# Down bias added by a product at the head of each expert block, and one expert block moved from second place to near the end

## The reference, cut to what matters

```python
def moe(x2, w_router, b_router, w_gate_up, b_gate_up, w_down, b_down):
    logits = (x2 @ w_router + b_router).astype(jnp.float32)
    top_v, top_i = lax.top_k(logits, TOP_K)              # 4 of 32
    gates = jax.nn.softmax(top_v, axis=-1)
    ...                                                  # tokens sorted by expert, in blocks
    def expert_block(args):
        xe, e = args
        gu = xe @ w_gate_up[e] + b_gate_up[e]            # 1024 x 2048
        gate, up = gu[:, :D_FF], gu[:, D_FF:]
        gate = jnp.minimum(gate, SWIGLU_LIMIT)
        up = jnp.clip(up, -SWIGLU_LIMIT, SWIGLU_LIMIT)
        h = gate * jax.nn.sigmoid(SWIGLU_ALPHA * gate) * (up + 1.0)
        return h @ w_down[e] + b_down[e]                 # 1024 x 1024
    ...
    return jnp.sum(y * gates[..., None].astype(y.dtype), axis=1)
```

## Time and profile before

| | us |
|---|---|
| median of three runs | 1329.43 |
| profiled execution | 1329.48 |
| its span, first to last instruction | 1327.6 |
| PE busy | 1227.2 (92%) |
| DVE busy | 826.2 (62%) |
| ACT busy | 608.1 (46%) |
| POOL busy | 147.5 (11%) |

### The profile page before, as it was taken

The page is one execution under the profiler, slowest core; times in us unless marked ns, Lnnn a source line. Parts: engine busy times, 40 slices in busy tenths (PEclk is TensorE's granted clock), DMA queues, the critical chain, the costliest instruction groups (busy, mean ns, idle before and its releaser), DMA issues.

```text
span 1327.6 us, 18587 instructions
## 1 busy us (share of the span) xinstructions
PE 1227.2 (92%) x6270; PEld 792.3 (60%) x6273; DVE 826.2 (62%) x1333; ACT 608.1 (46%) x822; POOL 147.5 (11%) x170
## 2 busy tenths in 40 slices
PE   7999999989999899999999999999999999999971
PEld 5888864467564647847474736574747747474620
DVE  3896758699382929929282837292829928374703
ACT  4111242387272727826263635272636736354502
POOL 9100012010000000000001010100010010101011
PEclk9999999989999999999999999999999999999987
DMA  9620178389999999999999999899999999999994
GB/s 320 92 42 1 38 231 335 130 297 402 354 416 411 419 412 418 413 407 418 408 419 400 419 391 375 320 416 417 419 411 420 393 386 419 408 421 382 424 401 179
DMA packets 67295, 457.49 MB, mean 345 GB/s; under 512 B 15758, under 2 KB 19538, under 8 KB 34456
## 3 DMA queue, kind: packets, MB, share of 16 engines
q1 hardware_dynamic: 56344, 435.28, 80.5%
q0 software_dynamic: 10880, 21.30, 6.8%
HBM read 439.99 MB, written 23.24 MB: 349 GB/s over the span
## 4 chain that ended last, share of the span: by engine, by line
PE 38%; DMA 21%; DVE 14%; issue 4%; ACT 2%; DVEq 0%; SPq 0%; ACTq 0%; POOLq 0%
PE bank L2270 20%; DMA ring_lo<-in_w_gate_up 17%; PE bank L2410 13%; DVE w_lo L2554 11%; DMA w_out<-in_w_down 4%; ACT w_hi L2048 1%; PE bank L2421 1%; DVE cmix L2572 1%; PE bank L2253 1%; PE bank L2260 1%; DVE h_lo L2567 1%; PE bank L2360 1%; DVE cmix L2575 1%; PE bank L2430 0%; DMA x<-token_sums 0%
## 5 line engine op out<-in xcount | busy, mean ns | idle before, releaser
L2554 DVE TENSOR_TENSOR w_lo<-ring_lo,w_hi 128x1024 fp32r<-128x1024 f32 x271 | 316.6, 1218 | 93.7 <-ACT w_hi L2048 91.7
L2048 ACT ACTIVATE w_hi<-ring_lo 128x1024 fp32r<-128x1024 f32 x271 | 271.1, 1052 | 86.4 <-DMA ring_lo<-in_w_gate_up 60.1
L2410 PE MATMUL bank<-ring_lo,x_s 128*64 128x512 f32 x832 | 187.4, 597 | 0.0
L2270 PE MATMUL bank<-w_hi,x_hi 128*128 128x512 f32 x544 | 175.2, 404 | 9.8 <-DVE x_lo L2560 7.7
L2270 PE MATMUL bank<-w_lo,x_hi 128*128 128x512 f32 x544 | 169.8, 393 | 0.0
L2270 PE MATMUL bank<-w_hi,x_lo 128*128 128x512 f32 x544 | 169.1, 392 | 0.0
L2554 DVE TENSOR_TENSOR w_lo<-w_out,w_hi 128x1024 fp32r<-128x1024 f32 x136 | 161.5, 1217 | 5.8 <-ACT w_hi L2048 5.7
L2048 ACT ACTIVATE w_hi<-w_out 128x1024 fp32r<-128x1024 f32 x136 | 141.1, 1055 | 30.8 <-PE bank L2270 30.7
L1943 POOL DMA_INDIRECT token_sums<-ymix,row_cur x32 | 54.0, 1688 | 725.7 <-ACT ymix L2078 700.3
L2270 PEld LDWEIGHTS bank<-w_hi,x_hi 128*128 128x128 f32 x544 | 99.1, 190 | 44.0 <-issue 19.4
L2410 PEld LDWEIGHTS bank<-ring_lo,x_s 128*64 128x64 f32 x832 | 56.2, 136 | 102.4 <-issue 100.5
(11 more groups left out here) (473 smaller groups left out, 1445.6 us busy)
## 6 DMA issues: line engine op xcount, KB each, us to landing
ring_lo<-in_w_gate_up SPq DMA_DIRECT2D x128, 2048.0 KB, 19.1
w_out<-in_w_down SPq DMA_DIRECT2D x128, 1024.0 KB, 20.7
ring_lo<-in_w_in SPq DMA_DIRECT2D x3, 2048.0 KB, 20.9
w_out<-in_w_out SPq DMA_DIRECT2D x2, 2048.0 KB, 9.6
x<-in_x_prompt SPq DMA_DIRECT2D x6, 512.0 KB, 11.6
ring_lo<-in_w_in SPq DMA_DIRECT2D x2, 1024.0 KB, 9.9
token_sums<-x SPq DMA_DIRECT2D x4, 512.0 KB
ffn_in<-hf SPq DMA_DIRECT2D x4, 512.0 KB, 5.5
```

Of the source, the lines that this page charges most:

```text
L2048: nc.scalar.activation(high(j), raw(j), ACT.Copy).then_inc(s["w_hi"], 1)
L2270: last = nc.tensor.matmul(bank[b + u][:], v[:, k, :], part(j)[:, u, :], start=(j == 16 and first), stop=(k == KD - 1 and part is high and ...
L2410: last = nc.tensor.matmul(bank[2 * half][64 * u:64 * u + 64, :], x_s[:, k % 4, 64 * (k // 4):64 * (k // 4) + 64], gu[:, k, :, half, 256 * ...
L2554: v.tensor_tensor(low(j), raw(j), high(j).bitcast(F32), ALU.subtract).then_inc(s["w_lo"], 1)
```

## The change

It has two parts.

**The down bias.** The gates' copies, their transposes, the ten products, ACT's copies over `x`, and POOL's five accumulating transfers are gone. Instead POOL splits `b_down` into three bf16 parts together with the gate/up bias (`bq` and `bparts` are 768 columns wide instead of 512, eight loads instead of four), stores them to HBM (`down_bias`, four more stores), and SP loads all 96 rows (3 parts of 32 experts) into a part of `x` that is free by then, ahead of the last two pieces of the first expert's weights. A 96 x 32 matrix `pick96` has, in the column of an expert, ones in the three rows of that expert. For each block DVE copies the expert's column to `picked_row` (`open_next`), and PE opens the block's down sums with a product of this column, broadcast over the slots, and the 96 bias rows (`open_down`): two bf16 matmuls of 512 columns for a wide or a small block, four of 256 for a quarter and for the rest beside position 16. The down products that follow no longer start the sums but add to them.

**The order.** The wide block at position 1 is gone from there: position 1 is now the small block of the first pair, and all that follows stands one position earlier. A wide block (`THIRD_EXTRA`, the smallest of the wide experts) stands at position 29, behind the last pair and ahead of the two quarters. The kinds and their numbers are as before, and so are the eight pieces of each expert and the rules for their issue.

```diff
-FIRST_EXTRA = 2 + 2 * PAIRS[0]
+FIRST_EXTRA = 1 + 2 * PAIRS[0]
...
-FINAL = SECOND_EXTRA + 2 + 2 * PAIRS[3]
+THIRD_EXTRA = SECOND_EXTRA + 1 + 2 * PAIRS[3]
+FINAL = THIRD_EXTRA + 2
...
+def down_rows(keep):
+
+    region = keep["x"][0:3 * E, NT - 1, :]
+    return tuple(region[:, o:o + n].bitcast(BF16) for o, n in ((0, D // 2), (D // 2, E // 2), (D // 2 + E // 2, 1)))
...
@@ router, SP @@
-        for c in range(P // E):
-            sp.dma_start(bdn[c * E:(c + 1) * E, :], a["b_down"][0]).then_inc(bdn_in, 16)
...
         sp.wait_ge(e["x_in"], 16)
+        sp.wait_ge(s["down_set"], 16 * 4)
+        sp.dma_start(down_rows(keep)[0], scratch["down_bias"].rearrange("r e c n -> (r e) (c n)")).then_inc(dn_in, 16)
         for j in range(6, LOADS):
             weight_load(sp, a, keep, mid, 0, j).then_inc(keep["landed"][j], 16)
@@ router, POOL @@
         for c in range(4):
-            pool.dma_start(bq[c * E:(c + 1) * E, :], a["b_gate_up"][0][:, c * 512:(c + 1) * 512]).then_inc(s["bias_in"], 16)
+            pool.dma_start(bq[c * E:(c + 1) * E, 0:512], a["b_gate_up"][0][:, c * 512:(c + 1) * 512]).then_inc(s["bias_in"], 16)
+            pool.dma_start(bq[c * E:(c + 1) * E, 512:768], a["b_down"][0][:, c * 256:(c + 1) * 256]).then_inc(s["bias_in"], 16)
...
+        pool.wait_ge(acc_set, acc_set0 + 16 * NT)
+        pool.wait_ge(s["fold"], 2)
+        g.tensor_copy(down_rows(keep)[1], pick96[:])
+        g.tensor_copy(down_rows(keep)[2][:, 0:1], pick96[:, 0:1]).then_inc(e["picked"], 1)
@@ experts, POOL @@
-        for q in range(3):
-            add_bias(q)
-        gather(1)
-        for q in range(3, NT):
-            add_bias(q)
-        pool.wait_ge(keep["bd_added"], 16 * NT)
+        gather(1, 2)
+        acc_set, acc_set0 = keep["spent"]["acc_set"]
+        pool.wait_ge(acc_set, acc_set0 + 16 * NT)
         scatter(0, 0)
@@ experts, PE @@
+        def open_down(b, parts=1):
+
+            n, step = P // parts, D // parts
+            for c in range(max(parts, 2)):
+                o, w = (0, 512) if parts == 1 else (n * c, step)
+                nc.tensor.matmul(bank[b + c if parts == 1 else b][o:o + n, 0:w], picked_row[:, 0:1].to_broadcast([3 * E, n]),
+                                 down_bias[:, c * w:(c + 1) * w], start=True, stop=False)
...
                 if j == 16:
+                    pe.wait_ge(s["y_free"], q + 1)
+                    open_down(4)
                     pe.wait_ge(s["h_lo"], 2 * lq + 1)
-                    pe.wait_ge(s["y_free"], q + 1)
...
-        wide(0, 0, expert_at(pe, 1), 1)
-        wide(1, 1, expert_at(pe, 2), 2)
+        wide(0, 0, expert_at(pe, 1), 2, True)
...
-        pair(3, PAIRS[3] - 1, 4)
+        pair(3, PAIRS[3] - 1, 1)
+        wide(THIRD_EXTRA, SMALL_RANK - 1, expert_at(pe, FINAL - 1), 4)
@@ experts, DVE @@
+        def open_next(e):
+
+            v.tensor_copy(picked_row[:, 0:1], pick96[:, bass.ds(e, 1)])
...
                 elif j == 23:
                     take_h(q, 1)
+                    open_next(e_next)
```

More of the change, by code:

```diff
@@ L1137, in router @@
     rest = buf("rest", [P, NT, E])
-    gate4 = buf("gate4", [P, NT, P // E, E])
-    gT = buf("gT", [P, NT * P])
-    bdn = buf("bdn", [P, D])
+    pick96 = buf("pick96", [3 * E, E], BF16)
     gsum = buf("gsum", [P, NT])
@@ L1179, in router @@
     keep["landed"] = [sem(f"landed{j}") for j in range(LOADS)]
-    keep["loop"] = {n: sem("e_" + n) for n in "onehot idx x_in xT_psum x_hi x_lo w_hi w_lo sel_psum bias_used".split()}
+    keep["loop"] = {n: sem("e_" + n) for n in "onehot idx x_in xT_psum x_hi x_lo w_hi w_lo sel_psum bias_used picked".split()}
     e = keep["loop"]
@@ L1275, in _ @@
         for c in range(4):
-            pool.dma_start(scratch["bias"][:, c], bparts[c * E:(c + 1) * E]).then_inc(s["bias_set"], 16)
+            pool.dma_start(scratch["bias"][:, c], bparts[c * E:(c + 1) * E, :, 0:512]).then_inc(s["bias_set"], 16)
+        for c in range(4):
+            pool.dma_start(scratch["down_bias"][:, :, c].rearrange("r e n -> e r n"), bparts[c * E:(c + 1) * E, :, 512:768]).then_inc(s["down_set"], 16)
         pool.wait_ge(s["bias_set"], 16 * 4)
+        pool.wait_ge(s["down_set"], 16 * 4)
         pool.wait_ge(s["mm"], 4 * NT)
@@ L1472, in _ @@
         x_transposes(Q)
-        pe.wait_ge(s["gate4"], Q)
-        for q in range(Q):
-            last = nc.tensor.transpose(bank[0][:, q * P:(q + 1) * P], gate4[:, q].rearrange("p c e -> p (c e)"), ident[:])
-        last.then_inc(s["gT_psum"], 1)
         strips(Q)
@@ L1479, in _ @@
         logits(Q)
-        pe.wait_ge(s["gT"], 1)
-        pe.wait_ge(bdn_in, bdn_in0 + 16 * (P // E))
-        for j in range(4):
-            bias_rows(j)
         ranks(Q)
@@ L1493, in _ @@
         last.then_inc(s["first_psum"], 1)
-        for j in range(4, 2 * Q):
-            bias_rows(j)
-        pe.wait_ge(s["gate4"], NT)
-        pe.wait_ge(keep["bd_sb"], 3)
-        nc.tensor.transpose(bank[3][:, 0:P], gate4[:, Q].rearrange("p c e -> p (c e)"), ident[:]).then_inc(s["gT_psum"], 1)
         pe.wait_ge(s["extra"], 1)
@@ L1501, in _ @@
         nc.tensor.matmul(bank[7][0:E, NT * E + 1:NT * E + 2], tri[0:E, 0:E], extra_b[:], start=True, stop=True).then_inc(s["upto_psum"], 1)
-        pe.wait_ge(s["gT"], 2)
-        for j in range(2 * Q, 2 * NT):
-            bias_rows(j)
         pe.wait_ge(s["held"], 1)
@@ L1515, in _ @@
                 last = nc.tensor.transpose(bank[XT_BANK[h]][:, (k % 4) * P:(k % 4 + 1) * P], xg[:, k * P:(k + 1) * P], ident[:])
-            last.then_inc(s["gT_psum"] if h == 0 else e["xT_psum"], 1)
-        pe.wait_ge(keep["bd_sb"], 9)
+            last.then_inc(s["x0_psum"] if h == 0 else e["xT_psum"], 1)
+        pe.wait_ge(s["x_new"], 2 * NT)
         pe.wait_ge(bias_in, bias_in0 + 64)
@@ L1809, in experts @@
     row_parts = {(n, c): scratch[n].rearrange("t (c d) -> (t c) d", c=c) for n in ("hf", "acc") for c in (1, 2, 4)}
+    down_bias, pick96, picked_row = down_rows(keep)
     def raw(j):
@@ L2012, in _ @@
         scatter_rest()
-        scatter(TOP, 0)
+        scatter(TOP, 1)
         with pool.Fori(0, PAIRS[2] - 1) as i:
-            pair(2, i, 1)
-        pair(2, PAIRS[2] - 1, 1, 1)
+            pair(2, i, 0)
+        pair(2, PAIRS[2] - 1, 0, 1)
         gather(SECOND_EXTRA + 1, 2)
         added(SECOND_EXTRA - 1)
-        scatter(SECOND_EXTRA, 1)
+        scatter(SECOND_EXTRA, 0)
         with pool.Fori(0, PAIRS[3] - 1) as i:
-            pair(3, i, 0)
-        pair(3, PAIRS[3] - 1, 0, 4)
+            pair(3, i, 1)
+        pair(3, PAIRS[3] - 1, 1, 1)
+        gather(THIRD_EXTRA + 1, 4)
+        added(THIRD_EXTRA - 1)
+        scatter(THIRD_EXTRA, 1)
         gather(FINAL, 4)
@@ L2179, in _ @@
             split(1, 0, j, first=True)
-        wide(0, 0, 0, 1, 1)
-        wide(1, 1, 1, 2, 2)
+        wide(0, 0, 0, 2, 1)
         def pair(run, i, side, next_parts=2):
@@ L2269, in products @@
                 for u in range(2):
-                    last = nc.tensor.matmul(bank[b + u][:], v[:, k, :], part(j)[:, u, :], start=(j == 16 and first),
+                    last = nc.tensor.matmul(bank[b + u][:], v[:, k, :], part(j)[:, u, :], start=False,
                                             stop=(k == KD - 1 and part is high and not first))
             last.then_inc(s["w_used"], 1)
+        def open_down(b, parts=1):
[4 more added lines that the diff above has]
+                                 down_bias[:, c * w:(c + 1) * w], start=True, stop=False)
         def set_bias(q):
@@ L2305, in set_bias_small, with wide @@
             last.then_inc(s["bias_used"], 1)
-        def wide(q, lq, e_next, next_parts):
+        def wide(q, lq, e_next, next_parts, first=False):
             pe.wait_ge(s["x_lo"], lq + 1)
@@ L2689, in _ @@
             split(0, j)
-        wide(0, 0, 0, expert_at(dve, 1), 1, blocks_back=0)
-        wide(1, 1, 1, expert_at(dve, 2), 2, 0)
+        wide(0, 0, 0, expert_at(dve, 1), 2, 0, blocks_back=0)
         def pair(run, i, side, next_parts=2):
```

172 lines of the change are left out of this document (74 added, 98 removed).

## The result

The changed kernel takes 1331.1 us (median of 18 runs, 1329.1 to 1334.8) where the kernel before, run beside it, takes 1328.23 (18 runs, 1327.02 to 1330.65): a ratio of 1.0022, 95% interval 1.0016 to 1.0029. The forecast was 0.9 us faster; it came out 2.9 us slower. The time lies in the range; the direction is wrong. The profiled execution (1333.17 us, span 1331.3) is one of the longer ones, by 2.1 us against the median; one part of the reason is shown further down.

The account below looks back on a forecast made before the run. The loop was taken as bound by DMA weight loads (411 GB/s), by compute where their share falls. Terms -0.7 + 1.5 - 0.2 - 2.2 + 0.7 = -0.9 gave 1328.5 us against the median; range 1324.5 to 1332.5.

Parts of the forecast that it names:

- Term B: Router: POOL's wider, later split holds up DVE, +1.5 us, between -2.7 and +5.5.
- term A: Router: without ten bias products the rank product starts sooner and DVE's `cum` waits less, -0.7 us, at most 0.98.
- the prediction's own sign: Router: PE's `x` transposes start about 1.5 us after 226.18; 224 or below means "faster", 229 or above "blocked in full on DVE".
- blocked in full on DVE: Router: every two-SBUF DVE step of the first tile ends only with a POOL step; +3.5, total 1330.6 us, chance 0.19.
- C: Block 0: four transposes instead of eight, one more short DVE step, two opening products; -0.2 us, between -0.5 and +0.5.
- D: Block order: position 1's wide block (35.8 us) goes, an extra wide near the end costs 33.6; -2.2 us.
- E: Opening products in other blocks: hidden by loads except at the largest expert's block and its rest; +0.7 us.
- faster: Rival: split's loss on DVE doesn't grow (-0.7), extra wide block costs less (-3.6); sum -4.5, 1325.0 us, chance 0.28.
- load queue: Rival: at position 29 the next load has lost its lead, leaving a gap; sum +4.2, 1333.7 us, chance 0.09.
- the products count: Rival: the loop is bound by PE, so opening products cost 14 us in all; about 1342 us, chance 0.04.

Follow-up runs that it names:

- the later turning: Changed kernel with the turning of the next block's token rows, ahead of the largest expert's block, moved behind two more pieces of down products: ratio 1.0012.
- the new order with the narrow split late: Kernel before with the new block order, POOL's adding transfers kept, and its 512-column gate/up split moved behind the sixth half tile of x: 0.9970, 1325.25 us.
- the whole split late: Changed kernel with POOL's whole split, gate/up and down bias together (768 columns), moved behind the sixth half tile of x: ratio 0.9975.

## Why the prediction was wrong

**Term B, the split, was the step that failed**, in its size: +1.5 was taken, +3.4 to +3.8 came. To the loop's start the old router needs 82.1 us (mean of 82.63 and 81.63), the router of the changed kernel 85.5 (mean of 85.06, 85.77, 85.99 with the later turning, 85.19), 3.4 more. To the end of the projections, where term A has no part yet, the same executions need 62.65 and 66.44 in the mean, 3.8 more. The prediction saw that "the steps also start later, since eight loads are to land and not four" and gave it half a microsecond; the trace of before already had four loads landing 0.8 to 1.5 us apart, and with the four more the start came 9.6 us later, out of the tables and into the chain of gates. There 4.5 to 5.3 us were lost in place of 1.6 to 1.8 (2.7 had been estimated). The rest, about 0.7 us from the sixth half tile to the end of the projections, goes with the half clock behind PE's 4.12 us wait, a consequence no term had: PE turns `x` at 228.42, 0.72 us after DVE's `x` is there, and before 0.06 us after it. By the prediction's own sign, PE's turning of `x` stands 3.3 us later behind the router's first instruction than before, which would be 229.5 for the 226.18 of the earlier trace rows, past the 229 named for the rival "blocked in full on DVE". By its size (+3.5) this is that rival, and its mechanism is the one seen; of the steps it named, two on `row` were held and `hf` was not, and casts and steps of the gates were held that it had not named.

**Term A, the bias products ahead of the rank product, was 0 at full clock, not -0.7.** The 0.98 us that `cum` waited in the earlier trace rows belong to one execution in which the clock had fallen. Its window, then the same place in the execution with the new order only, whose router is the same:

```profile
259.00:262.00 3.00, 3.00 (x11) 0.61 (x10) 2.04 (x9) 1.06 (x2) 0.00 (x0) 0.69 0.46 179
```

```profile
257.00:259.60 2.60, 2.54 (x11) 0.82 (x11) 2.36 (x9) 1.09 (x3) 0.00 (x0) 1.00 0.35 139
```

```profile
257.36 2.10 PE L1457 MATMUL bank<-bdn,gT 32*24 32x512 f32 x8
259.49 0.19 PE L1449 MATMUL bank<-mask_b,tri 128*128 128x32 bf16 x1
```

```profile
259.72 0.19 DVE L1647 SCALAR_TENSOR_TENSOR cum<-bank,mask_b 128x32 f32<-128x32 f32 x1 [0.18 <-PE bank L1449]
```

At full clock the eight products take 2.10 us in place of 2.97 and end together with the mask (259.46 and 259.44); `cum` waits 0.18, and 0.20 in the changed kernel without them. In the third profiled execution with this end of the router, the new order with the narrow split late, they take 2.10 too. A gain of 0.7 to 0.8 was there to be had in one execution of three. The reader of the earlier trace rows should have read the granted clock of that stretch first.

**Terms C and D held, and E is not resolved.** The order was to give 2.4 us with block 0 and gave 1.7 (interval 0.5 to 2.9); an extra wide at the end cost one load, with no dry queue there. C came out a little worse: block 0 takes 38.0 to 38.8 us in the new order, 38.1 before, where 0.2 less had been forecast; the granted clock of its first 5 us is 0.50 in the changed kernel, 0.72 before. E was put at +0.7: the nine loops in the new order with opening products take 1052.8 us in the mean and the three without them 1052.5, a difference far below the spread of the executions, and the version without the products was not faster at all. In the rival "faster", half-way to the bytes would be D = -3.7, not -3.6; nothing hangs on it. The rivals "load queue" and "the products count" did not come.

With 3.4 for A and B together, -1.7 for C and D as measured, and E as forecast, 0.7, the sum is +2.4 for a measured 2.9 with an interval of 2.1 to 3.9. A and B together had been put at +0.8; the 2.6 us between the two turned the forecast's direction.

## What to carry to other kernels

Work on GpSimd is not free when VectorE is on the path: ask which VectorE steps it will meet, which depends on when its data land, and put it where another engine is the bound; here one changed wait, three half tiles later, was worth some 2 us in the new order alone (0.9987 to 0.9970) and 6 in the changed kernel (1.0022 to 0.9975), more than the 2.9 that the change as a whole had cost. Before a wait is priced as a gain, read the granted clock of that stretch: here the wait behind products at half clock was there in one execution of three. And, when two traces are compared, count stages from their own first instruction.

## What the runs showed that was not expected

GpSimd and VectorE hold each other in both directions. In the kernel with the whole split late, DVE's `hf` (2.0 us undisturbed) took 3.48: it ended at 230.51, 1.80 behind the end of POOL's subtraction at 228.71. POOL's next cast, usually 0.82, then took 2.31 and ended 0.58 behind `hf`. So each seems to have waited for the other in turn, although the record of `hf` starts 0.04 us ahead of that of the subtraction:

```profile
227.07 1.64 POOL L1278 TENSOR_TENSOR bq<-bq,bparts 128x768 f32<-128x768 f32 x1
228.78 2.31 POOL L1276 CAST bparts<-bq 128x768 bf16<-128x768 f32 x1
```

```profile
227.03 3.48 DVE L1577 SCALAR_TENSOR_TENSOR hf<-x,row,gffn 128x1024 f32<-128x1024 f32 x1
```

Merging the eight small loads from POOL's queue into two did not make them land sooner: issued at 192.70 and 193.44 us, they landed at 213.19 and 218.87, where the eight of the changed kernel were all there at 210.37. The eight issued from SP, ahead of the first weights, were there at 198.42. Why the two large ones were so late was not tested.
